# A recurrent block whose gated output moves from VectorE to GpSimd and ScalarE

## The reference, cut to what matters

```python
ux = hx @ w_in
gx, rx = ux[..., :D_RNN], ux[..., D_RNN:]
rc = hc @ w_in[:, D_RNN:]
rx = centred_dwconv(rx, conv_w, conv_b); rc = centred_dwconv(rc, conv_w, conv_b)
for d in range(2):                       # forward and backward
    ac, bc = rglru_coeffs(rc, gate_w[d], gate_b[d], lam[d])
    ax, bx = rglru_coeffs(rx, gate_w[d], gate_b[d], lam[d])
    h_c = linear_scan(ac, bc, 0)         # h_t = a_t h_{t-1} + b_t
    h_x = linear_scan(ax, bx, h_c[:, -1])
yx = (gelu(gx) * (h_x[0] + h_x[1])) @ w_out
x = x + mx[:, :, 5] * yx
```

## Time and profile before

| | us |
|---|---|
| median of 3 runs | 3006.29 |
| lowest, highest | 2993.82, 3029.06 |
| the profiled execution, its own time | 2993.22 |
| its span in the profile | 2991.4 |
| PE, DVE, ACT, POOL busy | 2793.6, 1458.3, 780.3, 951.2 |

### The profile page before, as it was taken

The page is one execution under the profiler, slowest core; times in us unless marked ns, Lnnn a source line. Parts: engine busy times, 40 slices in busy tenths (PEclk is TensorE's granted clock), DMA queues, the critical chain, the costliest instruction groups (busy, mean ns, idle before and its releaser), DMA issues.

```text
span 2991.4 us, 39890 instructions
## 1 busy us (share of the span) xinstructions
PE 2793.6 (93%) x15091; PEld 2611.0 (87%) x15091; DVE 1458.3 (49%) x2331; ACT 780.3 (26%) x1008; POOL 951.2 (32%) x403
## 2 busy tenths in 40 slices
PE   6899999999988979999999899999997886899998
PEld 6899999998955779999999899999996775678886
DVE  6666456554333255554665522423217887232232
ACT  2322111112143232211111322111214666332222
POOL 1323223233311142232333322322234444444442
PEclk6899999999999989999999999999998898899998
DMA  5234434422300023434444122312221111233232
GB/s 192 84 112 127 115 106 122 126 78 68 106 6 16 29 75 106 132 105 115 112 115 131 36 63 82 107 49 63 73 60 36 53 53 50 70 91 105 86 107 67
DMA packets 413316, 256.67 MB, mean 86 GB/s; under 512 B 6637, under 2 KB 405830, under 8 KB 413254
## 3 DMA queue, kind: packets, MB, share of 16 engines
q1 hardware_dynamic: 413254, 255.87, 29.8%
HBM read 252.70 MB, written 4.25 MB: 86 GB/s over the span
## 4 chain that ended last, share of the span: by engine, by line
PE 80%; DVE 9%; ACT 4%; issue 4%; POOL 2%; DMA 0%; SPq 0%; DVEq 0%; ACTq 0%; POOLq 0%
PE pair_b L1420 30%; PE pair_a L1420 30%; PE pair_a L1410 2%; PE pair_a L1411 2%; PE pair_a L1412 2%; PE pair_b L1411 2%; PE pair_b L1412 2%; PE pair_b L1410 2%; PE pair_c L1452 2%; POOL w_lo L619 1%; DVE h_lo L1110 1%; PE pair_b L1643 1%; DVE neg_max L1305 1%; DVE sum_sq L1018 1%; DVE decay L1379 1%
## 5 line engine op out<-in xcount | busy, mean ns | idle before, releaser
L619 POOL TENSOR_TENSOR w_lo<-raw,w_hi 128x1024 fp32r<-128x1024 f32 (+3 forms) x302 | 829.8, 2748 | 1721.8 <-ACT w_hi L723 1721.8
L723 ACT ACTIVATE w_hi<-raw 128x1024 fp32r<-128x1024 f32 (+3 forms) x302 | 337.3, 1117 | 1363.2 <-PE pair_b L1420 493.0
L1000 DVE TENSOR_TENSOR work_g<-work_s,pair_b 128x768 f32<-128x768 f32 (+1 forms) x88 | 78.1, 887 | 706.9 <-PE pair_b L1420 546.2
L1420 PE MATMUL pair_a<-h_hi,w_hi 128*128 128x384 f32 x1408 | 370.0, 344 | 40.3 <-DVE h_lo L1110 29.0
L970 DVE SCALAR_TENSOR_TENSOR ada_sums<-ada_raw,cvec,ada_sums 128x256 f32<-128x256 f32 x896 | 397.7, 516 | 0.0
L1420 PE MATMUL pair_a<-h_lo,w_hi 128*128 128x384 f32 x1408 | 362.6, 338 | 0.0
L1420 PE MATMUL pair_a<-h_hi,w_lo 128*128 128x384 f32 x1408 | 361.6, 338 | 0.0
L1420 PE MATMUL pair_b<-h_hi,w_hi 128*128 128x384 f32 x1248 | 318.4, 336 | 6.0 <-POOL w_lo L619 6.0
L1420 PE MATMUL pair_b<-h_lo,w_hi 128*128 128x384 f32 x1248 | 318.0, 335 | 0.0
L1420 PE MATMUL pair_b<-h_hi,w_lo 128*128 128x384 f32 x1248 | 317.8, 335 | 0.0
L1420 PEld LDWEIGHTS pair_a<-h_hi,w_hi 128*128 128x128 f32 x1408 | 253.5, 191 | 52.7 <-issue 32.5
(11 more groups left out here) (275 smaller groups left out, 4242.4 us busy)
## 6 DMA issues: line engine op xcount, KB each, us to landing
raw<-in_ffn_w_gu_dram SPq DMA_DIRECT2D x176, 512.0 KB, 4.0
ada_raw<-in_ada_w_dram SPq DMA_DIRECT2D x64, 1024.0 KB, 5.2
raw<-in_ffn_w_down_dram SPq DMA_DIRECT2D x64, 704.0 KB, 4.8
raw<-in_rg_w_in_dram SPq DMA_DIRECT2D x20, 512.0 KB, 3.7
ada_first<-in_ada_w_dram SPq DMA_DIRECT2D x4, 2048.0 KB, 17.8
raw<-in_ab_w_in_dram SPq DMA_DIRECT2D x16, 512.0 KB, 3.9
raw<-in_rg_w_out_dram SPq DMA_DIRECT2D x8, 640.0 KB, 4.3
raw<-in_ab_w_out_dram SPq DMA_DIRECT2D x8, 512.0 KB, 3.7
```

Of the source, the lines that this page charges most:

```text
L619: nc.gpsimd.tensor_tensor(wl[:, par, 0:kt * P], raw[:, par, 0:kt * P], wh[:, par, 0:kt * P].bitcast(F32), ALU.subtract).then_inc(split_rea ...
L723: nc.scalar.activation(wh[:, par, 0:kt * P], raw[:, par, 0:kt * P], ACT.Copy).then_inc(hi_done, 1)
L1000: nc.vector.tensor_tensor(gbuf[:, 0, 0:W], sbuf[:, 0, 0:W], up, ALU.mult)\
L1420: last = nc.tensor.matmul(tokens(ps, a, a + HALF), w, of[:, k, a:a + HALF], start=begins, stop=ends)
```

## The change

DVE no longer makes the sum of the directions, y and the two casts. POOL gets `y_rows(n)`: the sum of the two directions into `yf`, then that times the gelu. ACT gets the casts as Copy activations: `conv_high(n)` behind `gelu_rows(n)`, `y_high(n-2)` behind `gelu_tanh(n-1)`. The factor 0.5 of y goes into the gate of the output projection: `coef_g` now gives the recurrent site 0.5 too. The wait of `gates` on ACT before it writes `decay` again is for the sum on POOL (`states_done`), not for y.

```diff
@@ POOL
+            def y_rows(n):
+                pool.wait_ge(scan_done, 2 * n + 2)
+                if n >= 1:
+                    pool.wait_ge(y_split, n)
+                nc.gpsimd.tensor_tensor(yf[:, :], decay[0][:, 0:SEQ], decay[1][:, 0:SEQ], ALU.add).then_inc(states_done, 1)
+                pool.wait_ge(states_done, n + 1)
+                pool.wait_ge(gelu_done, n + 1)
+                nc.gpsimd.tensor_tensor(yf[:, :], yf[:, :], gel[:, n % 2, :], ALU.mult).then_inc(y_done, 1)
@@ POOL, the list
                 low(p, (n + 1) % 2, KD)
                 low(p + 1, n % 2, 4)
                 if n == 1:
                     conv_low(0)
+                if n >= 2:
+                    y_rows(n - 2)
                 low(p + 2, (n + 1) % 2, KD)
                 if n >= 2:
                     y_low(n - 2)
                 conv_low(n)
             low(P_RG + 3 * KR - 1, 1, 4)
+            y_rows(KR - 2)
             y_low(KR - 2)
             low(P_RGOUT, 0, KR)
             low(P_RGOUT + 1, 1, KR)
+            y_rows(KR - 1)
             y_low(KR - 1)
@@ ACT, in gates(n)
                 if n >= 1:
-                    act.wait_ge(y_done, n)
+                    act.wait_ge(states_done, n)
@@ ACT
+            def conv_high(n):
+                act.wait_ge(conv_done, n + 1)
+                if n >= 2:
+                    act.wait_ge(panel_used, gate_panel(n - 2) + 1)
+                nc.scalar.activation(ch[n % 2][:, :], conv[n % 2][:, :], ACT.Copy).then_inc(conv_hi, 1)
+
+            def y_high(n):
+                act.wait_ge(y_done, n + 1)
+                nc.scalar.activation(yh[:, n, :], yf[:, :], ACT.Copy).then_inc(y_hi_done, 1)
@@ ACT, the list
             gelu_rows(0)
+            conv_high(0)
             for n in range(1, KR):
                 high(P_RG + 3 * n + 1)
                 u_rows(n)
                 gelu_tanh(n - 1)
+                if n >= 2:
+                    y_high(n - 2)
                 high(P_RG + 3 * n + 2)
                 gates(n - 1)
                 high(P_RG + 3 * n + 3)
                 gelu_rows(n)
+                conv_high(n)
 
             high(P_RG + 3 * KR + 1)
             gelu_tanh(KR - 1)
+            y_high(KR - 2)
             gates(KR - 1)
+            y_high(KR - 1)
@@ DVE, coef_g
-                nc.vector.tensor_scalar(mod_g[:, site, :, :], mods[:, t:t + KD, :], 1.0 if site % 3 == 1 else 0.5, None,
+                nc.vector.tensor_scalar(mod_g[:, site, :, :], mods[:, t:t + KD, :], 1.0 if site == 1 else 0.5, None,
@@ DVE, convolve(n)
-                dve.wait_ge(conv_done, n + 1)
-                if n >= 2:
-                    dve.wait_ge(panel_used, gate_panel(n - 2) + 1)
-                nc.vector.tensor_copy(ch[n % 2][:, :], conv[n % 2][:, :]).then_inc(conv_hi, 1)
@@ DVE, recur(n)
-                dve.wait_ge(scan_done, 2 * n + 2)
-                chain(nc.vector.tensor_tensor(decay[0][:, 0:SEQ], decay[0][:, 0:SEQ], decay[1][:, 0:SEQ], ALU.add))
-                if n >= 1:
-                    dve.wait_ge(y_split, n)
-                dve.wait_ge(gelu_done, n + 1)
-                nc.vector.scalar_tensor_tensor(out=yf[:, :], in0=gel[:, n % 2, :], scalar=0.5, in1=decay[0][:, 0:SEQ],
-                                               op0=ALU.mult, op1=ALU.mult).then_inc(y_done, 1)
-                dve.wait_ge(y_done, n + 1)
-                nc.vector.tensor_copy(yh[:, n, :], yf[:, :]).then_inc(y_hi_done, 1)
```

More of the change, by code:

```diff
@@ L355, in trunk @@
         scan_done = sem("scan_done")
+        states_done = sem("states_done")
         y_done = sem("y_done")
```

## The result

The changed kernel takes 3092.28 us (median of 4 runs, 3086.21 to 3106.49); the kernel before, run beside it, 3016.23 us (4 runs, 2993.82 to 3029.06). The ratio is 1.0267, 95% interval 1.0187 to 1.0347: some 80 us slower. The forecast was 3090 us, 84 us more. Runs of one kernel differ with the clock that PE was granted over the whole run: in a later set the kernel before took 2993.26 us at 0.961 and 3049.74 us at 0.936.

What follows compares the result with a forecast made beforehand. A loop of waits, with no engine full, was taken to pace the recurrent stretch. 9.1 + 67.0 + 8.5 = 84.6, say 84 us, added to the 3006.29 us median gave 3090 us, range 3050 to 3125.

Steps and rivals of the forecast that it cites:

- The deciding step, conv_hi on ACT: Recurrent blocks: conv_hi waits behind the gelu square, 8 us later, making a new loop of 34.5 us against 24.88.
- conv_hi to the u panel: Loop term: conv_hi copy 0.8, POOL's conv_lo and w_lo 5.6, hand-over to PE 0.2; 6.6 us.
- The u panel: Loop term: 48 products on PE, 8.3 us plus 2.8 of clock loss after idling; 11.1 us.
- Gates to the next conv_hi: Loop term on ACT: gate activations to the end of the gelu square and the next conv_hi; 11.4 us.
- first place: Start of the stretch: the u panel of block 2 starts at 2314.3 instead of 2305.24; +9.1 us.
- seven loops: Block 2 to block 9: 7 x 34.5 = 241.5 us instead of 174.5; +67.0 us.
- from u panel 9 to the last y product: End of the stretch, to the output projection: 65.1 us instead of 56.6, POOL's slower y on the path; +8.5 us.
- The clock term: u panel on PE: after some 10 us idle, 5.7 us run at the lower clock level, costing 2.8 us.
- Rival 1: u panel on PE: same loop at full clock, 31.7 us a block, 62 us more, 3068 us; chance 0.17.
- The port: DVE and POOL: they share an SBUF read port, so by that rule alone the time would hardly move.
- Rival 4: DVE and POOL: the port alone decides, -0.8 us a block, 8 us less, 2998 us; chance 0.03.
- rival 3: DVE's loop: relief comes through if conv_hi is in time, loop 21.5 us, 29 us less, 2977; chance 0.03.

Runs made afterwards that it cites:

- (2): Kernel before with only conv_hi moved to ACT behind the gelu square; sum, y and y_hi stay on DVE: 3086.25 us, ratio 1.0275 to the kernel before.
- (1): Changed kernel with conv_hi back on DVE; sum and y stay on POOL, y_hi on ACT: ratio 1.0021 to the kernel before.
- (3): Changed kernel with only POOL's list reordered, w_lo of the next u panel ahead of conv_lo; conv_hi stays late on ACT: ratio 1.0032 to the kernel before.
- (7): Changed kernel with conv_hi earlier on ACT's list, between gate tanh and decay: ratio 1.0019 to the kernel before.
- experiment 4: Changed kernel with 42 unused products on PE ahead of each u panel of blocks 2 to 9: ratio 1.0228 to the kernel before.
- (8): Changed kernel with two more 128x512 sums on POOL ahead of each y: period 34.04 us a block, single run, no ratio given.
- experiment 5: Changed kernel with conv_hi back on DVE and the u panel's w_lo ahead of conv_lo on POOL: 2994.45 us, ratio 0.9961 to the kernel before, again 0.9979.

## Why the prediction was right

**The deciding step, conv_hi on ACT.** Predicted: conv_hi 8 us later, and behind it on POOL conv_lo and the w_lo that PE waits for. Shown three ways: by its part alone (2), by undoing it (1), and by changing only what stands behind it (3) or ahead of it (7).

**The terms of the loop**, predicted and measured (timelines and chain above). conv_hi to the u panel 6.6, measured 2446.78 - 2440.72 = 6.1: conv_lo ran unhindered, 1.87 us for the 2.54 of the earlier trace rows, while w_lo took 3.23 for 3.12. The u panel 11.1, measured 11.3, behind 11.1 us of idle time. From its end to the gates 5.4, measured 2429.33 - 2424.16 = 5.2. Gates to the next conv_hi 11.4, measured 11.4. Sum 34.5 and 34.0.

**The sum.** Measured in the profiled executions: first place, from the first conv_lo to the u panel of block 2, 25.2 instead of 17.0 us, +8.2 (predicted 9.1); seven loops 2580.77 - 2345.32 = 235.5 instead of 174.5, +61.0 (67.0); from u panel 9 to the last y product 66.7 instead of 56.6, +10.1 (8.5); then +0.7. Together 80.0 against 84.6. The loops were overestimated by half a microsecond each through the 6.6, and by two u panels that ran 9.9 and 10.6 us instead of 11.3. The end was put too low, since a term of it was mis-sized. The gate products of the last block stood behind 10.65 us of idle time on PE and took 7.1 us, where the sum has 4.1; the clock loss had been counted for u panels alone. The stage table of these products:

```profile
2614.20:2621.30 7.10, 7.07 (x24) 5.79 (x24) 3.19 (x4) 0.00 (x0) 2.57 (x2) 0.58 0.32 92
```

DVE's last recurrence gave 0.9 us back (8.0 for 8.9), and POOL's y, y_hi and y_lo took the 4.7 us counted. These errors offset each other in part. That 3090 and 3092.28 lie 2 us apart is luck besides: the kernel before measured 3016.23 beside it and not the 3006.29 on which the forecast stands.

**The clock term** was taken from the row with the like idle time, and the stage table (5.97 us of the u panel at 0.50) and experiment 4 bear it out: it is 2.7 us of the u panel, and it goes when the idle time is filled. Rival 1 (full clock, 3068 us) is out.

**The port** was weighed too lightly, without harm here. Rival 4, the Trainium skill's sentence in Perfetto Trace Analysis, section Optimizing Scalar/DVE Operations, does not describe the changed kernel, whose y on POOL is hidden (8). But once the queue is right, it comes near: y's move gives 1.0 us a block of the 3.4 that rival 3 counted on, and nothing in experiment 1 beyond 0.3. Rival 3's condition, conv_hi in time for POOL's conv_lo, was as good as met in experiments 1 and 7 (POOL idles 1.52 and 1.80 us for it, and 4.92 in the kernel before), and its 21.5 us did not come. That step, "the loop is 21.0 plus 0.55", failed: a second loop and POOL's holds stood 0.4 to 1 us behind the first.

## What to carry to other kernels

When a small operation moves to another engine, price its place in that engine's list first: what must be done ahead of it, and what is queued behind whoever waits for it. Here a copy of 0.85 us cost 9 us a block, and one exchange in POOL's list took that back in the steady blocks, though not the 8.7 us of the first. Look then for the second loop before counting a gain: taking 3.9 us off the longest one gave 1.0.

## What was not expected of the hardware

Several DVE instructions that start while POOL runs an elementwise one show as busy until POOL is done: the y_hi cast, y_f and a scan took 2.51, 2.77 and 3.31 us for work of 0.43, 0.69 and 1.28. Not every one is held: the gelu step with `pair_b`, which lies in PSUM, took its usual 0.69 us at 2450.65, in the middle of POOL's w_lo of 3.09 us (experiment 5). The extra (2.0 to 2.1 us) stays with the moment, whether the cast, y_f, a scan or the sum stands there, so taking the held instruction away gains only its own time. The Trainium skill, SBUF — State Buffer, section Who interferes with whom, says that a DVE instruction with two inputs in SBUF contends with a GpSimd instruction that reads SBUF, and one with at most one such input, outside the two-port modes, does not. The rows agree: y_f, the sum and the scan have two inputs in SBUF, the gelu step one. In which mode the cast ran no run here shows.

Filling PE's idle time with 42 unused products shortened the block from 34.0 to 31.4 us, since the next panel then ran at the higher clock level throughout (8.60 us for its 48 products, granted clock of the block 1.00 instead of 0.80).
